# Prompt attention: the probabilities are turned by ordinary fp32 products with the identity

## The reference, cut to what matters

```
# NSA, per head h: three branches, each a masked softmax over keys, then times values
s_c = q . kc - slope * distance;  p_c = softmax(s_c);  o_c = p_c @ vc      # 16 compressed blocks
s_s = q . ks - slope * distance;  p_s = softmax(s_s);  o_s = p_s @ vs      # selected blocks (SLC)
s_w = q . kw - slope * distance;  p_w = softmax(s_w);  o_w = p_w @ vw      # window (WIN)
out = g0 * o_c + g1 * o_s + g2 * o_w
# DSA, per head h: keys chosen by an index score, top 128 for each query
score = sum_h w_h * relu(qi_h . ki);  sel = top_k(score)
p = softmax(q . k[sel] - slope * distance);  out = p @ v[sel]
```

## Time and profile before

| what | us |
|---|---|
| median of three runs | 2473.3 |
| lowest and highest of the three | 2473.27 and 2475.76 |
| the profiled execution's own time | 2475.57 |
| span in its trace | 2473.9 |
| PE busy in the span | 1899.8 |
| DVE busy | 984.8 |
| ACT busy | 322.0 |
| POOL busy | 257.9 |

### The profile page before, as it was taken

How to read it: one execution, slowest core, us unless ns; L and a number is a source line. 1 busy time by engine, 2 the same in 40 slices (tenths; PEclk the granted TensorE clock), 3 DMA queues, 4 the chain that set the end, 5 groups by cost and what they waited for, 6 DMA issues and landing times. The chain is left out here.

```text
span 2473.9 us, 53804 instructions
## 1 busy us (share of the span) xinstructions
PE 1899.8 (77%) x21662; PEld 1288.7 (52%) x21663; DVE 984.8 (40%) x2139; ACT 322.0 (13%) x754; POOL 257.9 (10%) x441
## 2 busy tenths in 40 slices
PE   4998268358888688745748998798898999999651
PEld 4886168244444577742435554454555655555320
DVE  3001855514667397934632222222222222222128
ACT  1000111014222110100101111111111111111000
POOL 0001000031000300000001111111111111111030
PEclk9999579567555555857859999898999999999875
DMA  9621000144100011208129999999999478997982
GB/s 314 230 86 31 4 6 1 42 188 177 61 0 1 1 37 41 97 3 307 52 114 412 412 412 413 414 368 412 412 410 402 171 315 321 413 412 311 415 318 92
DMA packets 132740, 533.73 MB, mean 216 GB/s; under 512 B 20300, under 2 KB 36705, under 8 KB 98131
## 3 DMA queue, kind: packets, MB, share of 16 engines
q1 hardware_dynamic: 111116, 475.18, 48.7%
q0 software_dynamic: 19952, 56.76, 6.0%
q10 hardware_dynamic: 1600, 0.79, 0.1%
HBM read 509.59 MB, written 25.08 MB: 216 GB/s over the span
## 5 line engine op out<-in xcount | busy, mean ns | idle before, releaser
L2431 PE MATMUL ps<-wgu,xTm 128*32 128x256 f32 x10112 | 612.3, 394 | 72.8 <-DMA wgu<-in_moe_wgu 71.6
L2431 PEld LDWEIGHTS ps<-wgu,xTm 128*32 128x32 f32 x10112 | 377.1, 113 | 266.8 <-issue 125.6
L2453 PE MATMUL ps<-wd,aT 128*32 128x256 f32 x5056 | 305.6, 382 | 16.0 <-DMA wd<-in_moe_wd 11.9
L2529 DVE TENSOR_TENSOR hx<-ps,biasT 128x256 f32<-128x256 f32 x158 | 67.1, 425 | 604.5 <-PE ps L2444 604.5
L2453 PEld LDWEIGHTS ps<-wd,aT 128*32 128x32 f32 x5056 | 163.0, 109 | 133.7 <-issue 65.0
L314 PE MATMUL ps<-hT,w_ring 128*128 128x260 f32 (+2 forms) x768 | 172.8, 386 | 2.0 <-DVE hT L356 2.0
L314 PEld LDWEIGHTS ps<-hT,w_ring 128*128 128x128 f32 (+2 forms) x768 | 140.6, 184 | 32.2 <-issue 4.8
L2499 ACT ACTIVATE gs<-ps 128x256 f32<-128x256 f32 x158 | 60.7, 384 | 639.1 <-PE ps L2431 639.1
L2549 DVE COPY orow<-ps 128x256 f32 x79 | 33.5, 425 | 199.0 <-PE ps L2453 199.0
L2387 POOL COPY gidx<-rowtok 128x1 int32 (+1 forms) x79 | 14.5, 183 | 855.5 <-PE ps L2418 855.5
L2383 POOL DMA_INDIRECT xg<-h_dram,gidx x79 | 79.7, 1009 | 64.6 <-POOL gidx L2387 64.6
(11 more groups left out here) (554 smaller groups left out, 2308.9 us busy)
## 6 DMA issues: line engine op xcount, KB each, us to landing
wgu<-in_moe_wgu SPq DMA_DIRECT2D x128, 2048.0 KB
wd<-in_moe_wd SPq DMA_DIRECT2D x64, 2048.0 KB
ada_ring<-in_w_ada SPq DMA_DIRECT2D x12, 2048.0 KB, 12.0
w_ring<-in_w_in SPq DMA_DIRECT2D x10, 1024.0 KB, 5.3
outbuf<-orow POOLq DMA_DIRECT2D x79, 128.0 KB, 8.6
outbuf<-zD SPq DMA_DIRECT2D x8, 512.0 KB
w_out_s<-in_w_out SPq DMA_DIRECT2D x2, 2048.0 KB, 10.2
xh<-in_x_prompt SPq DMA_DIRECT2D x1, 2048.0 KB
```

The lines of the kernel that those rows point to most:

```text
L2431: m = pe.matmul(ps[32 * c:32 * c + 32, p, 0:256].rearrange("r (s n) -> r s n", s=2), xT[:, t, 32 * q:32 * q + 32], wgu[b][:, 2 * q + t, :, ...
L2453: m = pe.matmul(ps[32 * c:32 * c + 32, 6, 0:256], aT[:, k, :], wd[b][:, k, 256 * c:256 * c + 256], start=(k == 0), stop=(k == KD - 1))
L2529: TT(h, ps[:, 2 + p, 0:256].rearrange("p (a n) -> p a n", a=8), b, ALU.add).then_inc(t_rd, 1)
```

## The change

At both places where the prompt attention turns probabilities, `pe.transpose` becomes `pe.matmul` with the same weights (the data), the same moving operand (the identity), the same target and the same semaphores. The lists of all five engines keep their instructions and their order; the line numbers behind line 1368 grow by one. There are 16 such calls at the starts of tiles (four for each tile) and 12 * (1 + 2 + 3 + 4) = 120 for the units.

```diff
@@ tile_start(i)
                 for h in range(HEADS):
-                    m = pe.transpose(ps[0:NB_P, 7, h * 128:(h + 1) * 128], pc[:, h, :], ident[:])
+                    m = pe.matmul(ps[0:NB_P, 7, h * 128:(h + 1) * 128], pc[:, h, :], ident[:], start=True, stop=True)
                 m.then_inc(c_mm, 1)
@@ turn(u)
                 for k in range(i + 1):
-                    m = pe.transpose(ps[:, 2 + u % 2, k * 128:(k + 1) * 128], P[:, u % 3, k * 128:(k + 1) * 128], ident[:])
+                    m = pe.matmul(ps[:, 2 + u % 2, k * 128:(k + 1) * 128], P[:, u % 3, k * 128:(k + 1) * 128], ident[:],
+                                  start=True, stop=True)
                 m.then_inc(t_mm, 1)
```

## The result

The changed kernel takes 2480.44 us (median of 20 runs, 2473.16 to 2485.35), the kernel before 2475.11 (20 runs, 2472.83 to 2477.45; the forecast rested on the first three of them). The ratio is 1.002, with a 95% interval of 1.0013 to 1.0027: slower by 0.2%, some 5 us. The forecast was 2482 (8.7 over the 2473.3 known then), with a range of 2475 to 2491. The profiled execution of the changed kernel took 2481.5 us; 1.7 us of it lie around its span of 2479.8.

A forecast was written before the change was run, and what follows sets the result against it. PE was taken to set the pace in tile 0 and the ends of tiles 1 to 3, at low clock. Terms 2.5 + 2.2 + 1.7 + 0.9 + 1.5 + 0 = 8.8 us; forecast 2482 us, range 2475 to 2491.

The forecast's parts named there:

- tile 0: Whole first tile of the prompt attention: PE full, part covered by waits for POOL; 2.2 us longer.
- starts of tiles 1 to 3: Four chained calls of line 1345 per tile, nothing beside them: 0.84 us for each tile, 2.5 us in all.
- tile 1, end: End of tile 1, where PE is full: 8 added passes, 1.7 us longer.
- tile 2, first eight: First eight units of tile 2: 2.9 us of added passes against 2.1 us slack; VectorE held up 0.9 us once.
- tile 2, end: End of tile 2, PE full: 12 added passes cost 2.5 us, given back by a clock rise one unit early.
- tile 3, first eight: First eight units of tile 3: added passes exceed VectorE's slack; between 0.9 and 3.0 us, taken as 1.5.
- tile 3, end: End of tile 3, all PE: 3.8 us of added passes, given back by an earlier clock rise; sum stays 17.9 us.
- The price of a call: Both changed lines: each call takes two passes instead of one, 0.21 us more at the low clock; 136 passes added.
- The cover in tile 1: First eight units of tile 1: VectorE is fuller, so PE's 2.54 us idle time hides 2.5 us of added passes.
- What the clock gives back: Ends of tiles 2 and 3: longer 128-row groups raise the clock sooner, giving back 2.5 and 3.8 us; not tiles 0, 1.
- The rival on turning passes: Full PE stretches: turning passes hold the clock down, ordinary products raise it; 2450 us, faster; chance 0.06.
- That what follows the stage would only slide along: Blocks after the prompt attention, parted by barriers: the stage's gain or loss reaches the end; changes beyond a few us contradict.

The follow-up runs named there:

- the five profiles with the short end of tile 3: Kernel before with 1, 3 or 5 idle VectorE instructions after the prompt attention, or (twice) 32 unused turning passes before the first key cache; stage 237.9 to 238.0 us.
- the delays: Kernel before with 1, 3, 5 or 22 idle VectorE instructions at the end of the prompt attention; 2474.12, 2472.17, 2475.58 and 2486.22 us.
- Turn twice: Kernel before with every turning pass at the two places done twice, no identity product; 2473.14 us, ratio 0.9989.
- the changed kernel with the warm passes: Changed kernel plus 32 unused turning passes of the identity in PE's wait before the first key cache; 2476.95 us, ratio 1.0008.
- the five profiles with added passes in the units: Changed kernel (twice), it with 32 unused turning passes, kernel before with turning passes doubled or only line 1368 changed; 2480.44, 2479.73, 2476.95, 2473.14, 2469.84 us.
- the eight with turning as before: Profiles of the kernel before: unedited, only line 1345 changed, four with idle VectorE instructions, two with 32 unused turning passes; 2462 to 2486 us range not given jointly.
- narrow: Kernel before with an ordinary product on 32 rows, overwritten, ahead of each turning pass of the units; 2553.69 us in one run.
- warm: Kernel before with 32 unused turning passes of the identity in PE's wait before the first key cache; 2463.99 us, again 2464.65.
- delay 1: Kernel before with one idle VectorE instruction at the end of the prompt attention; 2474.12 us, ratio 0.9987, runs in two groups.

## Why the prediction was right

The direction was right, and so was the mechanism: two passes for one, hidden in tile 1, paid where PE is full. The sizes were right in part by luck. For the stage 8.8 us were forecast and 9.0 measured, but six of its eight terms were off and made up for each other, and against the five profiles with the short end of tile 3 it would be 11.3. The total rose by 5.3 us and not by 8.7, because what follows the stage got shorter; that 2480.44 still lies so near to 2482 comes also from the kernel before, whose median was 2475.11 in 20 runs and not 2473.3 as in the first three.

| step | forecast | measured | 
|---|---|---|
| tile 0 | 2.2 | 3.0 (1.68 to V(8), 2.18 - 0.87 to V(12)) |
| starts of tiles 1 to 3 | 2.5 | 2.6 |
| tile 1, first eight units | 0 | 0.0 |
| tile 1, end | 1.7 | 2.1 |
| tile 2, first eight | 0.9 | 1.5 |
| tile 2, end | 0 (2.5 less what the clock gives) | 2.2 |
| tile 3, first eight | 1.5 | 0.0 |
| tile 3, end | 0 | -2.4, or 0 against the profiles of the delays |

*The price of a call* was mis-sized: 0.21 us for each block by the earlier trace rows. The steps inside a group are indeed 0.21, but each group of products costs about 0.11 more. In tile 1 a group of two blocks took 0.69 us as turning passes and takes 1.22; the same in tile 2, 0.90 and 1.65, in tile 3, 1.11 and 2.08. These are groups of tiles 1 and 2 before, then of tiles 1, 2 and 3 after:

```profile
667.68 0.69 PE L1368 MATMUL ps<-ident,P 128*128 128x128 f32 x2 [5.02 <-DVE P L1500]
...
733.02 0.90 PE L1368 MATMUL ps<-ident,P 128*128 128x128 f32 x3 [6.23 <-DVE P L1500]
```

```profile
656.74 1.22 PE L1368 MATMUL ps<-ident,P 128*128 128x128 f32 x4
...
756.16 1.65 PE L1368 MATMUL ps<-ident,P 128*128 128x128 f32 x6
...
811.32 2.08 PE L1368 MATMUL ps<-ident,P 128*128 128x128 f32 x8 [3.26 <-DVE P L1501]
```

The reason is in the weight loads (duration in ns: least, median, most; first and last start), before and after:

```profile
L1368 PEld LDWEIGHTS ps<-ident,P x120: 138/223/231, 601.9 to 828.3; 128*128 128x128 f32 x120
```

```profile
L1368 PEld LDWEIGHTS ps<-ident,P x240: 186/333/338, 602.4 to 837.2; 128*128 128x128 f32 x120
```

A load of 128 columns takes 333 ns for a product and 223 for a turning pass in the median. Inside a group the load runs beside the pass before it; the first of a group has no such pass. These are the first loads of a group in tile 3, before and after, 0.18 and 0.29 us:

```profile
812.55 0.18 PEld L1368 LDWEIGHTS ps<-ident,P 128*128 128x128 f32 x1 [9.16 <-DVE P L1500]
```

```profile
811.32 0.29 PEld L1368 LDWEIGHTS ps<-ident,P 128*128 128x128 f32 x1 [4.09 <-DVE P L1501]
```

The forecast took the unbroken products of line 684, in which there is no first. Its second source, eight products in 1.97 us, hid the difference: those have weights of 64 columns, whose load takes 227 ns in the median before, about as long as that of a turning pass. (For the end of tile 3 the prediction takes 1.86 us for a turn, elsewhere 1.97; measured are 2.08.) With 0.11 for each group, tile 0 gains 9 groups, 1.0, and the end of tile 1 four, 0.4, which is about what the table shows over the forecast. Turn twice agrees: its tile 0 gains only 0.21 for each pass (1.71 - 0.87 = 0.84 for four to V(12)).

*The cover in tile 1* held: VectorE's eight units take 31.18 us as before, and PE, which was idle for 2.5 of 20 us, has no idle time left.

```profile
641.00:661.00 20.00, 20.00 (x60) 12.34 (x59) 18.75 (x63) 5.66 (x18) 0.00 (x0) 0.50 0.00 1
```

*What the clock gives back* was right in that it comes in tiles 2 and 3, and wrong in its places and its worth. At the end of tile 2 it rose at 759.2 us, with the last output, and served only the next start: 0.97 us of PE work in 3.3 us. Of the 2.5 us forecast as given back there, 2.2 were paid.

```profile
759.30:762.60 3.30, 0.97 (x8) 0.87 (x8) 1.67 (x9) 0.26 (x1) 0.00 (x0) 1.00 0.00 0
```

In the changed kernel with the warm passes it did rise there in time, and the end of tile 2 took 29.58 us, less than the 31.85 of before. So the worth of that term changes between profiles of the same work. That it comes at all goes with the change: the five profiles with added passes in the units each have a rise in tile 2 or at its end, the eight with turning as before have none there (the clock of narrow stayed low). In the first eight units of tile 3 the clock was up three times, PE stayed ahead, and VectorE set the pace: 0 instead of 1.5.

*The rival on turning passes* is refuted: in warm the clock rises during turning passes alone, and in the changed kernel the full stretch of tile 0, with products in place of turning passes, stays at 0.50 (23.59 of 23.60 us busy). The sentence of the Trainium skill that it stood on ("TensorE: Matmul & The Clock Gate", Part 4: PE-mode transpose) does not hold in these traces.

*That what follows the stage would only slide along* was the step that failed. It was an assumption of the first paragraph, with no rival to it; the prediction named a change of a few us there as a sign of being wrong. What follows takes 1632.7 to 1645.4 us between profiles, and nearly all of that lies in the sample attention, by whether the clock is up at its two key caches. In the changed kernel's two profiles it is up at the first and low at the second, in the profile of before the other way round; the difference, 3.7 us in the sample attention and 2.9 in all that follows, offsets a part of the stage's 9.0. In the medians about 4 of 9 are offset, or 6 of 11.3. The delays show that the clock can rise at the first cache without a product. In the changed kernel five of the 20 runs have a mean granted clock of 0.819 to 0.823 and a median of 2477.0 us, the other fifteen 0.807 to 0.815 and 2481.15; with the warm passes, and the clock up at both caches in the profile, all have 0.819 to 0.823, and the median is 2476.95. It looks as if the five were of that kind, but they have no trace. What decides it stays open: only one run of a kernel has a trace, two of the changed kernel and of before with the warm passes.

## What to carry to other kernels

Turning blocks by ordinary fp32 products buys nothing: it is two passes for one, and a longer first weight load for each group; on a full PE both are paid in the stage. Before a difference of a few us is put down to a change, compare the untouched stages behind it, because the clock there can give or take ten us between runs of one kernel (delay 1). Where PE waits ahead of a long full stretch at the low clock, turning passes in the wait can bring the clock up for it, and it is worth a try; here they are worth 0.45 to 0.48%, more than the change cost.

## What the runs showed of the hardware

- The clock can rise during turning passes alone: in a group of 32 of them, 870.04 us on for 4.84 us, it went from 0.50 to 1.00 at 872.5.
- The load of 128 columns of fp32 weights takes 333 ns for a product and 223 for a turning pass in the median, and 0.29 and 0.18 us for the first of a group, at the low clock.
- A product of two passes on 32 rows and a turning pass on 128, in turn, cost 1.12 us a block, where three passes in a row would cost 0.63 (3 x 0.21): the weights are not loaded ahead across the change.
- The 272 passes at a key cache take 59 us where the clock is low and 32 to 34 where it is up; a rise at one of the two caches doesn't bring one at the other.
